# Modulation products of a two-model kernel: from row blocks summed on VectorE and TensorE to one accumulating VectorE product per 128 features

## The reference, cut to what matters

```
c_act = silu(c)                                    # 1 x 1024
ada = c_act @ ada_w[l] + ada_b[l]                  # ada_w: 1024 x 6144, so 6144 features
sh1, sc1, gt1, sh2, sc2, gt2 = split(ada, 6)
h = rmsnorm(x, norm1_g[l]) * (1.0 + sc1) + sh1
z = h @ w_in[l]                                    # latents, convolution input, gates
...
x = x + gt1 * y
h = rmsnorm(x, norm2_g[l]) * (1.0 + sc2) + sh2
x = x + gt2 * hierarchical_moe(h, ...)             # 32 experts
...                                                # the second model: the same with c_2, twice 3072 features
cos, sin = rope_tables(positions)                  # inv_freq 16 values, 256 positions
mask = positions[:, None, None, :] <= p_blk[:, None, :, None]
```

## Time and profile before

| | us |
|---|---|
| median of 3 runs | 1129.76 |
| lowest, highest run | 1128.46, 1139.05 |
| span of the profiled execution | 1125.3 |
| PE busy in it | 1045.9 (93%) |
| DVE busy | 672.3 (60%) |
| ACT busy | 531.0 (47%) |
| POOL busy | 503.0 (45%) |

### The profile page before, as it was taken

One profiled execution on the slowest core, in us unless ns is written; L12 is line 12 of the kernel. 1 busy time (PEld: TensorE's weight loads), 2 busy tenths in 40 slices (PEclk: granted clock), 3 DMA queues, 4 the chain that ended last, 5 costly groups with the idle time before them and its releaser, 6 DMA issues. The chain is left out here.

```text
span 1125.3 us, 20809 instructions
## 1 busy us (share of the span) xinstructions
PE 1045.9 (93%) x8330; PEld 921.9 (82%) x8330; DVE 672.3 (60%) x1425; ACT 531.0 (47%) x1171; POOL 503.0 (45%) x416
## 2 busy tenths in 40 slices
PE   6989989999989899998889999999899988999996
PEld 3787779888878788887788889899788978888885
DVE  5889783865746666676745535725545354555574
ACT  3534445204323322235685757656734544565543
POOL 0652351200535444654784664655442437455441
PEclk9999999999999999999999999999999998999999
DMA  9634325938499999633223222222211223333311
GB/s 366 237 107 189 113 75 204 395 136 337 189 372 346 399 387 390 265 117 139 103 87 114 76 76 77 81 109 79 111 39 39 76 84 125 132 113 117 146 39 38
DMA packets 25873, 186.27 MB, mean 166 GB/s; under 512 B 4145, under 2 KB 4913, under 8 KB 5681
## 3 DMA queue, kind: packets, MB, share of 16 engines
q1 hardware_dynamic: 24192, 184.77, 43.0%
q10 hardware_dynamic: 432, 0.18, 0.1%
q0 software_dynamic: 1152, 0.00, 0.1%
HBM read 196.47 MB, written 1.05 MB: 176 GB/s over the span
## 5 line engine op out<-in xcount | busy, mean ns | idle before, releaser
L3160 POOL TENSOR_TENSOR wL<-ring,wH 128x512 fp32r<-128x512 f32 x210 | 277.1, 1333 | 272.3 <-ACT wH L1614 271.9
L710 PE MATMUL bank<-xH,wH 128*128 128x256 f32 x832 | 257.5, 310 | 10.1 <-DVE xL L2267 3.4
L710 PE MATMUL bank<-xH,wL 128*128 128x256 f32 x832 | 237.0, 285 | 0.0
L710 PE MATMUL bank<-xL,wH 128*128 128x256 f32 x832 | 237.0, 285 | 0.0
L3160 POOL TENSOR_TENSOR wL<-ring,wL 128x512 fp32r<-128x512 f32 x79 | 107.6, 1382 | 172.1 <-ACT wL L1614 172.1
L710 PEld LDWEIGHTS bank<-xH,wH 128*128 128x128 f32 x832 | 160.7, 193 | 26.4 <-issue 12.6
L710 PEld LDWEIGHTS bank<-xH,wL 128*128 128x128 f32 x832 | 161.0, 193 | 5.2 <-issue 4.8
L710 PEld LDWEIGHTS bank<-xL,wH 128*128 128x128 f32 x832 | 160.7, 193 | 0.0
L1614 ACT ACTIVATE wH<-ring 128x512 fp32r<-128x512 f32 x264 | 155.3, 619 | 7.9 <-PE bank L710 5.3
L710 PE MATMUL bank<-ring,xg 128*128 128x256 f32 x640 | 146.0, 382 | 6.7 <-DMA ring<-in_exw 6.6
L2267 DVE SCALAR_TENSOR_TENSOR sz<-ring,cact,sz 128x512 f32<-128x512 f32 x154 | 139.4, 905 | 4.3
(11 more groups left out here) (226 smaller groups left out, 1919.3 us busy)
## 6 DMA issues: line engine op xcount, KB each, us to landing
ring<-in_wts SPq DMA_DIRECT2D x123, 1024.0 KB, 6.0
ring<-in_exw SPq DMA_DIRECT2D x32, 1536.0 KB, 10.4
ring<-in_wts SPq DMA_DIRECT2D x1, 1152.0 KB, 5.2
xT<-in_xT SPq DMA_DIRECT2D x1, 1024.0 KB, 13.4
out<-hT SPq DMA_DIRECT2D x4, 256.0 KB, 2.5
cst<-in_cst SPq DMA_DIRECT2D x1, 800.0 KB, 6.3
ring<-in_wts SPq DMA_DIRECT2D x1, 640.0 KB, 4.2
vec<-in_vec SPq DMA_DIRECT2D x1, 217.5 KB, 5.6
```

Source lines behind the costliest of these rows:

```text
L710: return pe.matmul(o, l, r, start=start, stop=stop, skip_group_check=True)
L3160: return pool.tensor_tensor(o, x, h.bitcast(F32), ALU.subtract)
```

## The change

The modulation weights are laid out transposed: a chunk `ada{j}a` or `b` now holds 256 output features, feature on the partition, with all 1024 inputs of each along the free dimension. The condition, silu applied to all 1024 values, stands on every partition (`conds`), brought by a transfer that repeats the row 128 times. One `tensor_tensor_reduce` per 128 features multiplies, sums over 1024 places, starts from the bias and writes one column of `adaT`; the products themselves overwrite the chunk. PE's `columns`, `direct` and `stand`, ACT's `row_out`, DVE's `close` and the 16 condition columns of `vec` go; two `warm` calls on PE change their counts. The chunks keep their size, their place and their order. `positions` moves from DVE to POOL: its steps there are `tensor_scalar` and `tensor_tensor`, the part up to the angles ahead of POOL's first low part of a weight, the mask part after that of `in0`.

```diff
+    def half(j, x):
+        if j < 12:
+            add(f"ada{j}" + "ab"[x], "ada_w", None, (512 * j + 256 * x, 512 * j + 256 * x + 256))
...
+        conds = (sz[:, :, :].rearrange("p i n -> p (i n)"), tmp2[:, :])
...
@@ tensor_program @@
-            direct(0, "a")
-            direct(0, "b")
-            stand(0)
             for k in range(8):
                 stat(0, k, 0)
-            cols.append(2)
-            columns()
-            warm(3, 6)
+            warm(3, 4)
             conv_in(0, 0, range(4))
-            direct(1, "a")
-            direct(1, "b")
-            conv_in(0, 1, range(2))
-            cols.append(3)
-            columns()
-            stand(1)
-            conv_in(0, 1, range(2, 4))
+            conv_in(0, 1, range(4))
+            warm(3, 8)
             conv_in(1, 0, range(4))
...
-                for _ in range(matvec_steps(u)):
-                    next(gad, None)
...
@@ scalar_program @@
+            act.dma_start(conds[0], ins["c"].broadcast_to([128, D])).then_inc(l_c.up(0), 16)
             act.dma_start(posb, ins["pos"].broadcast_to([128, T])).then_inc(l_pos.up(0), 16)
...
+            e.wait_ge(l_c, 0)
+            fn(conds[0], conds[0], ACT.Silu).then_inc(silu_c.up(0))
...
+            e.wait_ge(turn_d, (4, 2))
+            act.dma_start(conds[1], ins["c2"].broadcast_to([128, D])).then_inc(l_c.up(1), 16)
...
@@ vector_program @@
+            def matvec(j, x):
+                name = ada_name(j) + "ab"[x]
+                w = raw(name, 2)
+                e.wait_ge(loaded(name), name)
+                e.wait_ge(silu_c, j // 12)
+                e.wait_ge(l_vec, 0)
+                for i in range(2):
+                    f = 4 * j + 2 * x + i
+                    dve.tensor_tensor_reduce(w[:, i, :], w[:, i, :], conds[j // 12], 1.0, vcol("ada_b", f), ALU.mult, ALU.add,
+                                             adaT[:, f:f + 1]).then_inc(ada_d.up((j, 2 * x + i)))
+                    yield
...
-            pos_ = positions()
-            for n, _ in enumerate(ada(2)):
...
+            for x in range(2):
+                each(matvec(0, x))
+                each(matvec(2, x))
             normed_half(0)
             split.need("cv0b")
-            each(ada(3))
-            close()
...
+            for x in range(2):
+                each(matvec(3, x))
+                each(matvec(1, x))
             normed_half(1)
-            each(pos_)
...
@@ gpsimd_program @@
+            pos_ = positions()
+            next(pos_)
             split.need("cv0b")
...
             each(beside(split, "in0", nothing))
+            each(pos_)
```

245 lines of the change are left out of this document (75 added, 170 removed).

## The result

| | before | changed |
|---|---|---|
| median of 20 runs, us | 1133.75 | 1137.23 |
| lowest, highest | 1128.46, 1140.04 | 1134.55, 1146.49 |
| PE busy in the profiled execution | 1045.9 | 1024.1 |
| DVE busy | 672.3 | 639.0 |
| POOL busy | 503.0 | 540.7 |

The ratio of the changed kernel to the one before is 1.0043, 95% interval 1.0025 to 1.0061, so +4.9 us (2.8 to 6.9). The forecast was 1125.5 with a range of 1115 to 1135, on a median of 1129.76 of three runs; over 20 runs the same kernel's median is 1133.75. PE has 22 us less work and DVE 33, and the kernel is slower.

What follows compares the result with a forecast made beforehand. PE's time was taken to bound the kernel, with DMA a second limit between 338.9 and 460 us. +6 - 4.5 - 5.5 = -4.0 on 1129.8 gave 1125.8, rounded to 1125.5; range 1115 to 1135.

Steps and rivals of the forecast that it cites:

- Term 1, the start: Start up to the second convolution half: tables on POOL delay PE by 9.4, less PE work and cold clock; +6 us.
- The meeting with DVE: At the start, DVE's eight two-input products slow POOL's table steps by a quarter over 10 us: 2.5 us.
- case C: DVE and POOL exclude each other: eight products, 11 us, all go on top; start about +14, 1134 us; chance 0.15.
- PE's removed work, -5.5: Before the second convolution half, PE loses 9.3 us of work and gains 3.8 of warming products: net -5.5.
- covered: DVE's second batch of eight products and `normed_half(1)`, ready near 48.5, finish before PE wants them at 53.
- Cold clock, +2: PE reaches its first convolution product after some 12 us without work; about 4 us at half speed cost +2.
- Nothing on the path but up to +1: POOL's mask part meets DVE's taps for some 2 us; nothing on the path but up to +1.
- Term 2, the price: DVE's new product over 1024 places with its sum costs 1.4 us; DVE's saving is priced at nothing.
- Case D: DVE's product with the sum runs at half rate, 2.5 us each; sum +16.5, 1146 us; chance 0.08.
- Term 3: Output projections: six column sums leave PE, five worth 4.05 us and the sixth 0.45; -4.5 us.
- Term 4: Experts: fourteen column sums of 0.90 us leave PE; between 2.7 and 6.3 us gained, taken as -5.5.
- The lower bound of 2.7: Experts: 2.7 us was the least gain forecast, against 6.3 at most.

Runs made afterwards that it cites:

- e10: The changed kernel with DVE's first eight products over 128 of their 1024 places (some modulation columns wrong); 1132.2 us, 0.9986 of the kernel before.
- e13: The changed kernel with 38 instead of 4 warming products on PE ahead of the convolution's first piece; 1135.6 us, 1.0019 of the kernel before.
- e7: e6 with one group of DVE's taps moved behind the copy of the last latent; 1129.6 us, 0.9951 of the kernel before.
- e1: The changed kernel with the tables and mask part (`positions`) back on DVE; 1131.3 us, 0.9982 of the kernel before.
- e6: e1 with positions loaded ahead of the condition and all table steps at the front of DVE's program; 1130.9 us, 0.9977 of the kernel before.
- e12: e7 with 21 instead of 8 warming products on PE between the two convolution pieces; 1124.2 us, 0.9914 of the kernel before.
- e2: The changed kernel with POOL's tables moved behind the low parts of `in0`, ACT's two Sin ahead of `qkv()`; 1134.9 us, 1.0007 of the kernel before.
- e8: The changed kernel with the positions loaded ahead of the condition on ACT's queue; 1132.3 us, 0.9978 of the kernel before.
- e9: e7 with only half of each of the 28 modulation chunks between the experts loaded (some columns wrong); 1121.7 us, 0.9901 of the kernel before.
- e14: The changed kernel with positions loaded first, `warm(3, 20)` for `warm(3, 4)`, and taps as in e7; 1127.0 us, 0.9947 of the kernel before.
- e3: The kernel before with only the tables and mask part moved from DVE to POOL; 1137.2 us, 1.0041 of the kernel before.

## Why the prediction was wrong

**What bounds the kernel: right in the main, wrong in the size at the start.** PE's time pays in the projections and at the end of the experts. At the start PE waits, and what counts there is the meeting of POOL and DVE.

**Term 1, the start, failed.** Forecast +6; by the traces `in0` starts 8.6 us later and `qkv` 11.8 later (with 3.4 us more half clock in the latter's share). Step by step:
- Positions at about 10: 9.55. Right. The chain without DVE's products, 20.7 + 2.4 = 23.1: 21.7 in e10. Right, so 32 partitions cost what 128 do.
- The meeting with DVE, taken as 2.5: 29.9 - 21.7 = **8.2**. This is the mis-sized step, 5.7 too little; the shorter chain and the earlier positions gave 1.9 of it back, and PE started at 41.23 for the 37.3 of the forecast. Beside the eight products the chain lost 4.9, twice what I had said: I had put POOL's median of 1.24 for 0.92, measured beside plain two-input steps with pauses between, on a stretch in which DVE runs products end to end. The other 3.3 I had not seen at all: the longer chain also met the normalisation and the second batch. The maxima of the earlier trace rows said more than the medians. The Trainium skill's page "SBUF — State Buffer", section "Who interferes with whom", says more still; by its rule (a full lock) the 10.2 us of the eight products would all be added, and the runs show 4.9. The other way round, products beside POOL's low parts take 2.27 to 2.29 for 1.27. My case C, which held the full exclusion for 0.15, gave 1134 and so comes nearest to the time, though its full exclusion isn't what the runs show.
- PE's removed work, -5.5: right in the changed kernel. From the first product of one piece to that of the other it needs 16.5 us for 21.3, and in e13, without the half clock, 15.0. PE was the limit there only because POOL was so late ("covered" was right too). It is no gain of the change by itself: once the tables were away, PE waited 6.2 us between the pieces (e7), and the second piece began 1.4 to 2.0 us later than before (e1, e6), behind eight products of DVE that need 12.3 us there instead of the 7.4 of before.
- Cold clock, +2: in the first piece itself 3.7 us at half clock, so about 1.8. Right. e13 gives 2.7 in all, and e12 4.2: idle time at the start seems to cost clock later too.
- The latents had no term. From `in1` to `qkv` the changed kernel needs 21.5 us for 16.9: DVE's taps beside POOL's low parts and mask part took 10.58 us for 16, and a half clock from 92.7 to 99.5 fell into it. "Nothing on the path but up to +1" was wrong; e2 and e7 show that DVE's taps are on it.

**Term 2, the price, was right.** 1.27 + 0.08 = 1.35 for 1.4. Case D, half rate, is refuted: the Trainium skill's page "Vector Engine (DVE) Microarchitecture Reference", section "Points that are easy to get wrong", speaks of half throughput for `S2S2D2_STT` with two SBUF sources that are not bf16; the trace does not agree for this instruction, which takes 1.24 ns per place, where the plain step took 1.47 at 512.

**Term 3, -4.5: right.** From `wo` to the router 72.1 before, 68.1 in e1, e2, e8 and e13, none with a half clock in it: -4.0. In the changed kernel's own trace one costs it back (69.8).

**Term 4, -5.5: half.** The stage is 228.3 before and 225.6 in the changed kernel, e7 the same: -2.7. By the three windows: -2.3 for the 3.6 of the first four sums, **+2.3** where I had let the middle take back 0.9 and give 0.9, and -2.7 as forecast at the end. The holes that a faster PE left were filled with waiting for chunks (6.6 to 14.8 us), whose pace is set by bytes (e9) and, as far as argued, by when they are issued. The lower bound of 2.7 would have been the value to take: in this stage, with 95% on the DMA engines, less work elsewhere gained nothing.

**The sum again:** the start and latents about +10 (11.8, less the greater share of half clock, an estimate from these traces), -4.0 and -2.7 make +3.3 against 4.9 measured; the more frequent half clock of the later stages fits in the rest, which isn't settled more finely than that. Against the forecast, these single traces put the misses at 2.6 us in the start, 3.2 in the latents, 0.5 in the projections and 2.8 in the experts: 9.1 with the half clock in them, where -4.0 forecast and +4.9 measured are 8.9 apart. That the time lies outside the range is in part the base: on the 1129.8 of three runs +4.9 would be 1134.7, inside it by luck, with the sign wrong all the same.

## What to carry to other kernels

An engine's idle time is a place for work only if the work does not slow the engine that the path goes through. Price the meeting of DVE's two-input steps with POOL's from the maxima of such rows, not from medians: here 10.2 us of products lengthened POOL's chain by 4.9. Then ask what the longer chain will meet next (3.3 us more here). Work taken off PE while it waits for another engine is worth nothing. And a wait of PE has a price of its own: the granted clock was at half in or behind the waits of 16.4 us (the change), 6.2 (e7) and 3.6 (e14), and filling one of them with idle products was the cheapest gain here (4.2 us, with intervals that overlap a little). A large load put ahead of a small one in a queue delays whoever needs the small one: here the positions came at 9.55 instead of 6.06, and two lines in another order were worth 7.4 us. Before a difference below 1% is explained, compare the mean clocks.

## What the runs showed of the hardware

- A DVE product of two SBUF inputs with accumulation over 1024 places costs 1.27 us alone, 1.40 beside POOL's `TENSOR_SCALAR` on 32 partitions, 1.49 beside that on 128 and 2.27 beside its `TENSOR_TENSOR` of 128x512; POOL's low part of 128x512 takes 1.44 in e3 and 1.84 beside the products.
- POOL's steps on 32 partitions cost what they cost on 128: `TENSOR_TENSOR` 0.72 and 0.73; `TENSOR_SCALAR` 0.92 in both where the factor comes from a tile (e10, at 9.97; the earlier trace rows), and 0.85 on 32 where it is a constant.
- The mean granted clock differed between kernels by up to 0.011 (0.973 to 0.984) and moved with PE's idle time at the start. Between kernels with the same work (e7 and e12, the change and e13) 0.0036 and 0.008 went with 4.2 and 2.7 us; most of the latter's 0.008 is the idle stretch itself. Between executions of one kernel 0.001 went with 0.8 us.
